# A two-layer decoder step on one core: the weight sums of the gate's chunk on VectorE, and a new order beside the heads

## What is computed

```python
qa, ka, va, qi, ki, wi, qb, kb, vb, gb = jnp.split(z, splits, axis=-1)   # z = h @ w_in[l]
qb = rope(qb.reshape(B, T, H_B, HEAD_DIM), pos)
kb = rope(kb.reshape(B, T, H_B, HEAD_DIM), pos) * (HEAD_DIM ** -0.5)
...
a = mixer_a(qa, ka, va, qi, ki, wi)            # softmax attention over the selected keys
o, S = retention(qb, kb, vb, s0)               # chunks of 128 tokens, with a running state
o = group_norm(o) * g_ret_l * silu(gb)
m = jnp.concatenate([a, o], axis=-1) @ w_out[l]
```

## Time and profile before

| | before |
|---|---|
| median of 3 runs | 1586.56 us (1582.09 to 1586.9) |
| the profiled execution | 1585.04 us, span of its trace 1583.3 us |
| TensorE busy | 1544.6 us, 98% |
| VectorE busy | 830.5 us, 52% |
| GpSimd busy | 506.6 us, 32% |
| ScalarE busy | 457.5 us, 29% |

### The profile page before, as it was taken

The page is one execution under the profiler, slowest core; times in us unless marked ns, Lnnn a source line. Parts: engine busy times, 40 slices in busy tenths (PEclk is TensorE's granted clock), DMA queues, the critical chain, the costliest instruction groups (busy, mean ns, idle before and its releaser), DMA issues.

```text
span 1583.3 us, 21882 instructions
## 1 busy us (share of the span) xinstructions
PE 1544.6 (98%) x8062; PEld 1173.3 (74%) x8062; DVE 830.5 (52%) x1688; ACT 457.5 (29%) x1059; POOL 506.6 (32%) x398
## 2 busy tenths in 40 slices
PE   8999999999999999999999999999999999999998
PEld 5445666588888888888844466665888888888887
DVE  4698686755653003332467977848465520133334
ACT  5222355224421002310252224561253210032101
POOL 0005320213654324444320062201236524233461
PEclk9999999999999999999999999999999999999999
DMA  6426311023331222212223272110243321222211
GB/s 205 139 67 214 134 55 50 7 84 107 133 132 54 107 97 89 80 55 105 78 87 107 80 241 81 54 54 2 85 133 134 114 98 54 107 96 91 80 54 54
DMA packets 52812, 150.42 MB, mean 95 GB/s; under 512 B 8250, under 2 KB 29506, under 8 KB 39394
## 3 DMA queue, kind: packets, MB, share of 16 engines
q1 hardware_dynamic: 45218, 140.65, 25.7%
q10 hardware_dynamic: 7488, 8.36, 1.6%
HBM read 139.79 MB, written 9.02 MB: 94 GB/s over the span
## 4 chain that ended last, share of the span: by engine, by line
PE 74%; DVE 20%; ACT 3%; issue 2%; DMA 0%; POOL 0%; ACTq 0%; DVEq 0%; POOLq 0%
PE ps L1192 46%; PE ps L1130 7%; PE ps L849 7%; PE ps L810 5%; DVE arena L1885 3%; DVE top L1883 3%; PE ps L775 1%; DVE x_feat L2034 1%; DVE arena L1829 1%; DVE arena L1831 1%; PE ps L990 1%; PE ps L1000 1%; DVE rstd_ffn L1825 1%; PE ps L977 1%; DVE rstd_ffn L1827 1%
## 5 line engine op out<-in xcount | busy, mean ns | idle before, releaser
L1192 PE MATMUL ps<-arena,wring 128*128 128x256 f32 (+1 forms) x1280 | 285.8, 382 | 0.3 <-DVE arena L2118 0.3
L1192 PEld LDWEIGHTS ps<-arena,wring 128*128 128x128 f32 x1280 | 243.0, 190 | 37.8 <-DVE arena L2118 1.1
L810 PE MATMUL ps<-wring,h_feat 128*128 128x512 f32 (+1 forms) x576 | 256.1, 584 | 2.4 <-ACT h_feat L1315 2.1
L2430 POOL TENSOR_TENSOR wring<-wring,arena 128x512 f32<-128x512 f32 (+1 forms) x48 | 78.7, 1639 | 346.7 <-PE ps L1192 323.4
L810 PEld LDWEIGHTS ps<-wring,h_feat 128*128 128x128 f32 x576 | 102.8, 190 | 110.0 <-issue 96.7
L1192 PE MATMUL ps<-h_feat,wring 128*128 128x256 f32 (+1 forms) x768 | 176.6, 381 | 0.0
L1192 PEld LDWEIGHTS ps<-h_feat,wring 128*128 128x128 f32 x768 | 145.9, 190 | 21.6
L1192 PE MATMUL ps<-mix,wring 128*128 128x256 f32 (+1 forms) x512 | 120.2, 383 | 1.5 <-DVE p_sb L2092 1.5
L1192 PE MATMUL ps<-arena 128*128 128x264 f32 x512 | 119.2, 386 | 0.0
L1130 PE MATMUL ps<-mix,wring 128*128 128x256 f32 (+1 forms) x512 | 115.1, 384 | 0.8 <-ACT mix L1484 0.8
L2413 POOL TENSOR_TENSOR pt_sb<-pt_sb 128x256 f32<-128x256 f32 (+1 forms) x94 | 72.9, 775 | 125.1 <-ACT pt_sb L1289 121.8
(11 more groups left out here) (252 smaller groups left out, 2166.5 us busy)
## 6 DMA issues: line engine op xcount, KB each, us to landing
wring<-in_w_all SPq DMA_DIRECT2D x108, 1024.0 KB, 5.0
arena<-in_cache_k SPq DMA_DIRECT2D x32, 256.0 KB, 5.3
arena<-in_cache_v SPq DMA_DIRECT2D x32, 256.0 KB, 4.1
o_k_out<-arena ACTq DMA_DIRECT2D x2, 1024.0 KB
o_v_out<-arena ACTq DMA_DIRECT2D x2, 1024.0 KB
arena<-in_state SPq DMA_DIRECT2D x2, 1024.0 KB, 4.9
o_rets_out<-arena ACTq DMA_DIRECT2D x2, 1024.0 KB, 10.3
wring<-in_w_idx SPq DMA_DIRECT2D x3, 648.0 KB, 5.0
```

The costliest lines, as they stand in the source:

```text
L810: last = mm(ps[:, bank_of(c, i), 0:width], h_feat[:, k, token_cols(t)], wt, start=(k == 0), stop=(k == KD - 1))
L1192: last = mm(out, a[:, j, :], b, start=(opens(n) and j == 0), stop=(j == nk - 1), skip_group_check=True)
L2430: nc.gpsimd.tensor_tensor(dst, in0, in1, op).then_inc(s_ready, 1)
```

## The change

It has five parts, the same in both layers.

1. The four weight sums of chunk 6 go from GpSimd to VectorE: `weight_sum(n)`, one instruction of 1,024 columns each, after head steps 20, 22, 24 and 26. TensorE waits for them on a semaphore of their own.
2. GpSimd's remaining sums (chunks 4 and 5, and all input sums) are made in four instructions of 256 columns in place of two of 512.
3. On VectorE the block sums of a chunk stand ahead of a block's first head step (`ahead`), no longer behind it. The rotations are spread so that two never stand behind neighbouring steps: the sample tile of chunk 4 is rotated before head step 0, that of chunk 5 after step 13. `own_values(1)` is one step earlier.
4. On ScalarE, sigmoids 1 to 4 stand one by one between copies of transposed groups, and on VectorE all five `gate_mult` stand together before `decay_scores(0)`.
5. The four small DMAs are issued by SP, behind weight unit 17, and wait there for chunk 7's sample tile to be evacuated.

```diff
+                for u in range(12, 18):
+                    unit(u)
...
+                sp.wait_ge(rope_done, past(rope_done) + 5 * TILES)
+                sp.wait_ge(proj_read, past(proj_read) + read_base(7) + 1)
+                sp.dma_start(qr[:], zq).then_inc(bounce, 16)
+                sp.dma_start(kr[:], zk).then_inc(bounce, 16)
+                for j in range(2):
+                    sp.dma_start(vr[j:P:2, :], vv).then_inc(bounce, 16)
+                for u in range(18, UNITS):
...
-                take_groups([qT[:, h, :] for h in range(4)])
-                gate_sigmoid(1)
-                take_groups([kT[:, h, :] for h in range(4)])
+                take_groups([qT[:, 0, :], qT[:, 1, :]])
+                for n in range(1, TILES):
+                    gate_sigmoid(n)
+                    take_groups([(qT[:, 2, :], qT[:, 3, :], kT[:, 0, :], kT[:, 1, :])[n - 1]])
+                take_groups([kT[:, 2, :], kT[:, 3, :]])
...
-                gate_sigmoid(2)
-                gate_sigmoid(3)
-                gate_sigmoid(4)
...
+            def ahead(c, i):
+
+                if i == 7:
+                    chunk_c12(c)
+                if i == 0:
+                    chunk_c21(c - 1)
+                if i == 4:
+                    chunk_u2(c)
+                if c > 4 and i == 6:
+                    chunk_u3(c)
+                    chunk_c22(c)
+
+            def weight_sum(n):
...
+                a11, a12, a21, a22 = (chunk_block(6, which) for which in ("11", "12", "21", "22"))
+                dst, in0, in1_, op = {1: (cs1, a21, a22, ALU.add), 2: (cs2, cs1, a11, ALU.subtract),
+                                      3: (a21, a11, a21, ALU.subtract), 4: (a12, a12, cs2, ALU.subtract)}[n]
+                v.tensor_tensor(dst, in0, in1_, op).then_inc(gate_sums, 1)
+                dve.wait_ge(gate_sums, up(gate_sums))
+
+            sums_beside = {(6, 0, 0): 1, (6, 1, 0): 2, (6, 2, 1): 3, (6, 3, 1): 4}
+            turns = {(5, 0, 1): (4, 2), (5, 2, 0): (4, 3), (5, 3, 0): (4, 0), (5, 4, 0): (4, 1), (5, 5, 0): (5, NT),
+                     (6, 0, 1): (5, 2), (6, 2, 0): (5, 3), (6, 3, 0): (5, 0), (6, 4, 0): (5, 1)}
...
-                gate_mult(0)
+                for n in range(TILES):
+                    gate_mult(n)
                 decay_scores(0)
-                gate_mult(1)
-                gate_mult(2)
                 sample_state(0)
-                gate_mult(3)
-                gate_mult(4)
                 sample_state(1)
...
-                for e in (slice(0, 2), slice(2, 4)):
+                for e in range(4):
                     nc.gpsimd.tensor_tensor(dst[:, e], in0[:, e], in1_[:, e], op).then_inc(chunk_sums, 1)
                     pool.wait_ge(chunk_sums, up(chunk_sums))
...
-                for n in range(1, 5):
-                    chunk_sum(6, n)
```

More of the change, by code:

```diff
@@ L449, in build @@
         in_sums = sem("in_sums")
+        gate_sums = sem("gate_sums")
         chunk_sums = sem("chunk_sums")
@@ L716, in _ @@
                 sp.dma_start(st, layer(state, "a p n -> (a p) n")).then_inc(state_in, 16)
-                for u in range(12, UNITS):
+                for u in range(12, 18):
+                    unit(u)
+                zq = zr[1][0:NB, NT, :].rearrange("b (r d) -> b r d", d=32)
+                zk = zr[0][0:NB, NT, :].rearrange("b (r d) -> b r d", d=32)
+                vv = v_tok[0:NB, NT, :].rearrange("b (r d) -> b r d", d=HD)
+                sp.wait_ge(rope_done, past(rope_done) + 5 * TILES)
[5 more added lines that the diff above has]
+                for u in range(18, UNITS):
                     unit(u)
@@ L817, in project, with sums_here @@
                     between(i, KD - 1)
+            def sums_here(c, n):
+                if c == 6:
+                    pe.wait_ge(gate_sums, past(gate_sums) + n)
+                else:
+                    pe.wait_ge(chunk_sums, past(chunk_sums) + 4 * (4 * BLOCKED.index(c) + n))
             def project_blocks(c, between):
@@ L827, in project_blocks @@
                     if n == 6:
-                        pe.wait_ge(chunk_sums, past(chunk_sums) + 2 * (4 * q + 2))
-                        pe.wait_ge(in_sums, past(in_sums) + 2 * 2)
+                        sums_here(c, 2)
+                        pe.wait_ge(in_sums, past(in_sums) + 4 * 2)
                     if n == 5 and c == 6:
-                        pe.wait_ge(in_sums, past(in_sums) + 2 * 5)
+                        pe.wait_ge(in_sums, past(in_sums) + 4 * 5)
                     if n == 7:
-                        pe.wait_ge(chunk_sums, past(chunk_sums) + 2 * (4 * q + 3))
-                        pe.wait_ge(in_sums, past(in_sums) + 2 * 3)
+                        sums_here(c, 3)
+                        pe.wait_ge(in_sums, past(in_sums) + 4 * 3)
                     if n == 3:
-                        pe.wait_ge(chunk_sums, past(chunk_sums) + 2 * (4 * q + 4))
+                        sums_here(c, 4)
                     if n == 4:
-                        pe.wait_ge(in_sums, past(in_sums) + 2 * 4)
+                        pe.wait_ge(in_sums, past(in_sums) + 4 * 4)
                     for k in range(KD):
@@ L1618, in _ @@
                 scale_quad(6, "21", proj_c21)
-                take_groups([qT[:, h, :] for h in range(4)])
-                gate_sigmoid(1)
-                take_groups([kT[:, h, :] for h in range(4)])
+                take_groups([qT[:, 0, :], qT[:, 1, :]])
[3 more added lines that the diff above has]
+                take_groups([kT[:, 2, :], kT[:, 3, :]])
                 act.wait_ge(out_v, past(out_v) + 32)
                 evacuate(7, 0)
-                gate_sigmoid(2)
-                gate_sigmoid(3)
-                gate_sigmoid(4)
-                zq = zr[1][0:NB, NT, :].rearrange("b (r d) -> b r d", d=32)
-                zk = zr[0][0:NB, NT, :].rearrange("b (r d) -> b r d", d=32)
-                vv = v_tok[0:NB, NT, :].rearrange("b (r d) -> b r d", d=HD)
-                act.dma_start(qr[:], zq).then_inc(bounce, 16)
-                act.dma_start(kr[:], zk).then_inc(bounce, 16)
-                for j in range(2):
-                    act.dma_start(vr[j:P:2, :], vv).then_inc(bounce, 16)
                 evacuate(7, 1)
@@ L2162, in own_values @@
                 dve.wait_ge(om_ready, up(om_ready))
+            def ahead(c, i):
[9 more added lines that the diff above has]
+            def weight_sum(n):
+                if n == 1:
+                    for u in (12, 13):
+                        dve.wait_ge(w_slot[u % SLOTS], past(w_slot[u % SLOTS]) + 16 * (u // SLOTS + (u % SLOTS >= 2)))
+                    dve.wait_ge(chunk_sums, past(chunk_sums) + 4 * 4 * 2)
+                    dve.wait_ge(proj_done, past(proj_done) + product_at(5, 5))
+                if n == 3:
+                    dve.wait_ge(proj_done, past(proj_done) + product_at(6, 0))
+                if n == 4:
+                    dve.wait_ge(proj_done, past(proj_done) + product_at(6, 2))
+                a11, a12, a21, a22 = (chunk_block(6, which) for which in ("11", "12", "21", "22"))
[3 more added lines that the diff above has]
+                dve.wait_ge(gate_sums, up(gate_sums))
@@ L2283, in _ @@
                 chunk_c22(4)
+                rope(4, NT)
                 for c, i in ATT_BLOCKS:
                     steps = head_steps(c, i)
+                    ahead(c, i)
                     for s, (slot, step) in enumerate(steps):
```

49 lines of the change are left out of this document (7 added, 42 removed).

## The result

The changed kernel takes 1559.84 us, median of 4 runs (1558.32 to 1562.12), beside 1585.28 us for 4 runs of the kernel before (1582.09 to 1586.9): ratio 0.9843, 95% interval 0.9821 to 0.9865. It is faster, by 25.4 us, where 18.9 us and a time of 1567.7 us were forecast.

A forecast was written before the change was run, and what follows sets the result against it. TensorE, busy 1544.6 of 1583.3 us, bounds the kernel, so only its 38.7 us idle can be gained. Removed waits of 12.9 + 2.7 + 3.3 = 18.9 us take 1586.56 to 1567.7 us; range 1562 to 1578 us.

The forecast's parts named there:

- the six waits: TensorE waits, both layers: mask 7.5, heads 2.6 and 2.0, bank 0.8, evacuated v 2.7, finished chunk 3.3 us; all go.
- none behind the mask: Rival, 22%: VectorE's lag partly returns; chunk 6's 2.60 us mask wait stays in both layers, 1572.9 us.
- none for the finished chunk: Rival, 9%: waits only move; earlier TensorE waits for VectorE's chain at turn and output projection, 1582.6 us.
- Of itself that buys no time: Part 1: VectorE gains 4.9 us of sums, loses 6 us of contention per layer; balance -1 us, near nothing.
- the step that looked for the sums' contention in chunk 6: Part 1: each of eight GpSimd sum instructions can delay VectorE some 1.0 us; at most 8, taken 6 us per layer.
- 12.9 us were counted: Part 3, beside the heads: TensorE's waits of 7.5 + 2.6 + 2.0 + 0.8 us counted as gone, both layers.
- 2.7 + 3.3 = 6.0 us were counted: Parts 4 and 5, behind the heads: waits for evacuated v (2.7 us) and the finished chunk's turn (3.3 us) go.
- The 2.0 us of the turn's gain: Behind the heads: DMAs no longer behind sigmoids, so VectorE's start at 291.01 comes some 2.0 us earlier.
- the sum: Removed TensorE waits added up over both layers: 12.9 + 2.7 + 3.3 = 18.9 us gained.
- a busy time of still 1544 us: Sign of being right: changed profile shows TensorE busy still 1544 us in a span of about 1564.
- the base: Starting time 1586.56 us, the median shown for the kernel before, from which 18.9 us were subtracted.
- The clock: TensorE's granted clock falls to 0.50 near 148 us, costing about 2 us; a second fall is covered by the range.

The follow-up runs named there:

- the swap alone: The kernel before, old order kept, with only the four weight sums of chunk 6 moved from GpSimd to VectorE: 1584.0 us, ratio 0.9998.
- order alone: The kernel before with only VectorE's new order, plus a VectorE wait for GpSimd's last sum ahead of decayed keys: 1576.85 us, ratio 0.9955.

## Why the prediction was wrong in size

**What bounds the kernel, and the six waits: right.** All six groups went at once, and no rival's wait came: none behind the mask, none for the finished chunk.

**Part 1: the price right, the verdict half right.** The sum costs 1.23 us (taken 1.21), and what GpSimd's four cost VectorE is 5.9 us a layer (taken 6), though part of it fell on normalisings, which the forecast counted at their undisturbed time. "Of itself that buys no time" is shown by the swap alone, ratio 0.9998. But the step that looked for the sums' contention in chunk 6 looked in the wrong place for two of the four. Sums 1 and 2 run at 203.97 and 206.67 in the kernel before, in chunk 5, and move to 199.6 with an earlier TensorE, straight under a rotation. With the new order and no other part they cost 3.04 us a layer, and a fall of the clock behind it 1.50 us more in one of the two. The forecast never asked what a faster TensorE does to the start of GpSimd's sums. Parts 1 and 2 each cover this, so the result did not show the gap.

**Part 2: right to cost GpSimd's longer sums at nothing.** They are longer than forecast, 3.2 to 3.9 us in place of 2.9: a quarter of a sum takes 0.8 us or more, where the one row behind the 0.73 us was another addition. No matmul waits for them. What a rotation instruction loses was right (0.4 to 0.5 us). That quarters matter for the waits is shown only without part 1: with it, halves cost 0.2 us a layer.

**Part 3: mechanism and margins right, term too small.** 12.9 us were counted; the steps give 7.16 + 7.17 = 14.3 us, the whole stretches 14.7.

**Parts 4 and 5: right, term too small.** 2.7 + 3.3 = 6.0 us were counted; the steps give 6.5, the whole stretches 6.7. The turn of the finished chunk was right with no margin in place of 0.5 us. The 2.0 us of the turn's gain were put down to the DMAs no longer standing behind the sigmoids. That holds, but moving the sigmoids does it alone; the move to SP is not needed.

**One step that failed is the sum**: it took the idle time that the profile shows for a wait as the time that its removal gives back. Each wait gave 0.07 or 0.08 us more, or 0.16 to 0.20 us. The timeline shows where this comes from: the four score matmuls at 206.98 are put at 0.92 us, to 207.90, but the next begin at 207.83. The idle time in brackets counts from the recorded end of the matmul ahead. Without the wait the next one starts 0.07 to 0.16 us before that end, and this is what the bracket misses. The ends of matmuls are modelled in this profile, so it says how to read the bracket, not what the engine does in that time. Over seven waits a layer this is 0.8 us, and a step of 0.13 us at 203.8, whose cause is open, comes on top: 10.4 in place of 9.4 us, 1.9 us in both layers. With the smaller steps behind them it is 2.5 us. It is also a part of the 5.3 us that TensorE's busy time lost, where the forecast's sign was a busy time of still 1544 us.

**The other, and the largest term, is the base: a median of three runs.** 1586.56 us stands against 1583.75 for 41 later ones: 2.8 us too high. The clock was named, but priced as a fall more and only for the range; "about 2 us" for a fall was too much as well (1.7 us by the trace, 1.4 by the fit), and fewer falls, about 0.9 per run by the mean clock, give 1.3 us. The first set of the changed kernel lies 0.9 us under the median of its eight runs. So of the 7.9 us of error, 2.8 are the base, 1.9 to 2.5 the sum, 1.3 the clock and 0.9 the draw; 1.0 to 0.4 us stay open. The mechanism was right and the sizes were not. The range reached down by 5.7 us for the spread of the runs and the transposes, and the base alone had used half of it.

## What to carry to other kernels

Subtract the starts of the same instructions in two traces: the steps show what each wait was worth, apart from falls of the clock, which show as runs of small steps; and each wait was worth a little more than the idle time in brackets. When TensorE is made faster, look for every engine that is released by it and ask what it will now lie on top of: here GpSimd's sums slid 4 us forward onto a rotation. Spread the rotations first; shorter GpSimd instructions and work moved to VectorE bought 2 us and nothing alone, and either one was enough beside the order, but for 0.2 to 0.4 us a layer. A base of three runs is no base for an effect of one per cent.

## What the runs showed of the hardware

- The granted clock falls to 0.50 in one trace and not in another at the same instruction: ten matmuls of 256 columns took 3.86 us before and 2.43 us in the changed kernel, after waits of 0.27 and 0.21 us. Two traces of the changed kernel differ in the same way (a stretch at 0.50 from 145.6 us, and none). So do the two layers of order alone, after waits of 2.97 and 2.96 us. The mean clock of a whole run, to three digits, sorts the runs of one kernel by time, 1.4 us for each 0.001.
- A VectorE instruction of two SBUF inputs loses a large part of the GpSimd instruction that is under way: 0.95 to 1.09 us under halves of 1.3 us (0.43 became 1.52, 0.69 became 1.64), 0.4 to 0.5 under quarters (0.69 became 1.10). The normalising, one tile and one column of reciprocals, loses as much (0.42 became 1.48). The masks, which read PSUM, lose nothing (0.42 us for 256 columns, under GpSimd and clear of it).
- Four DMA issues on ScalarE take 2.7 us (274.82 to 277.54), and cost nothing where it waits for TensorE anyway.
